# Two value projections by seven block products, and the gate sums of the linear attention moved behind them

## The reference, cut to what matters

```python
# stage "v": stick-breaking attention of the first block
q, k, v = jnp.split(x @ w_qkv, 3, axis=-1)      # v: 512 x 1024
# stage "od_v": gated linear attention of the second block
z = h @ w_in
q, k, v, r, ga = jnp.split(z, [hk, 2 * hk, 2 * hk + hv, 2 * hk + 2 * hv], axis=-1)   # v: 512 x 1024
log_a = jax.nn.log_sigmoid((ga @ w_a2 + b_a).astype(jnp.float32)) / C_TAU
b = jnp.cumsum(log_a, axis=3)                   # within chunks of 64 tokens
q_t, k_t, k_s = q * jnp.exp(b), k * jnp.exp(-b), k * jnp.exp(b_last - b)
```

## Time and profile before

| | us |
|---|---|
| Median of 3 runs | 2387.3 (2385.33 to 2389.44) |
| The profiled execution's own time | 2386.84 |
| Its span in the profile | 2385.0 |
| PE busy | 2340.6 (98%) |
| PEld busy | 2037.7 (85%) |
| DVE busy | 1587.9 (67%) |
| ACT busy | 1029.4 (43%) |
| POOL busy | 339.0 (14%) |

### The profile page before, as it was taken

One profiled execution on the slowest core, in us unless ns is written; L12 is line 12 of the kernel. 1 busy time (PEld: TensorE's weight loads), 2 busy tenths in 40 slices (PEclk: granted clock), 3 DMA queues, 4 the chain that ended last, 5 costly groups with the idle time before them and its releaser, 6 DMA issues.

```text
span 2385.0 us, 36878 instructions
## 1 busy us (share of the span) xinstructions
PE 2340.6 (98%) x14899; PEld 2037.7 (85%) x14899; DVE 1587.9 (67%) x2174; ACT 1029.4 (43%) x1352; POOL 339.0 (14%) x294
## 2 busy tenths in 40 slices
PE   7699999999999999999999999999999999999999
PEld 7688899988886678999878779999888877899987
DVE  8845877846536777777585546899534545799942
ACT  6421544532225725445234444556423344455622
POOL 6402000002002240000224241000121002000000
PEclk9899999999999999999999999999999999999999
DMA  2422333233232122332333313233332212333332
GB/s 58 104 97 90 105 107 105 83 101 113 89 99 69 40 94 85 107 103 82 96 107 110 89 64 114 82 105 89 101 102 85 93 66 71 89 107 107 85 107 85
DMA packets 328844, 219.67 MB, mean 92 GB/s; under 512 B 11188, under 2 KB 319050, under 8 KB 328618
## 3 DMA queue, kind: packets, MB, share of 16 engines
q1 hardware_dynamic: 322298, 208.46, 29.6%
q0 software_dynamic: 3024, 7.90, 1.4%
q10 hardware_dynamic: 3360, 1.02, 0.2%
HBM read 206.59 MB, written 2.10 MB: 87 GB/s over the span
## 4 chain that ended last, share of the span: by engine, by line
PE 90%; DVE 4%; POOL 3%; ACT 2%; issue 1%; SPq 0%; DMA 0%; DVEq 0%; ACTq 0%; POOLq 0%
PE psum L1380 9%; PE psum L1382 9%; PE psum L1381 9%; PE psum L1136 9%; PE psum L1138 9%; PE psum L1137 9%; PE psum L1349 3%; PE psum L1350 3%; PE psum L1351 3%; PE psum L1524 2%; PE psum L1525 2%; PE psum L1526 2%; PE psum L1248 1%; PE psum L1244 1%; PE psum L1245 1%; PE psum L1228 1%
## 5 line engine op out<-in xcount | busy, mean ns | idle before, releaser
L2093 ACT CAST w_hi<-w_stage 128x2048 fp32r<-128x2048 f32 x129 | 246.7, 1912 | 691.8 <-PE psum L1138 408.4
L2973 DVE TENSOR_TENSOR w_lo<-w_stage,w_hi 128x2048 fp32r<-128x2048 f32 x126 | 300.0, 2381 | 275.6 <-ACT w_hi L2093 275.6
L1380 PE MATMUL psum<-x_sum_hi,w_hi 128*128 128x256 f32 x1088 | 308.0, 283 | 0.2 <-issue 0.2
L1382 PE MATMUL psum<-x_sum_hi,w_lo 128*128 128x256 f32 x1088 | 307.9, 283 | 0.0
L1381 PE MATMUL psum<-x_sum_lo,w_hi 128*128 128x256 f32 x1088 | 307.9, 283 | 0.0
L2163 ACT CAST w_hi<-w_parts 128x1024 fp32r<-128x1024 f32 x204 | 213.3, 1049 | 200.9 <-PE psum L1382 111.1
L3101 DVE TENSOR_TENSOR w_lo<-w_parts,w_hi 128x1024 fp32r<-128x1024 f32 x204 | 248.1, 1219 | 51.7 <-ACT w_hi L2163 50.5
L1380 PE MATMUL psum<-x_hi,w_hi 128*128 128x256 f32 x816 | 230.9, 283 | 0.0
L1381 PE MATMUL psum<-x_lo,w_hi 128*128 128x256 f32 x816 | 230.9, 283 | 0.0
L1382 PE MATMUL psum<-x_hi,w_lo 128*128 128x256 f32 x816 | 230.9, 283 | 0.0
L1136 PE MATMUL psum<-hidden_raw_hi,w_hi 128*128 128x512 f32 x572 | 223.6, 391 | 0.3 <-DVE w_lo L2973 0.3
(11 more groups left out here) (584 smaller groups left out, 5283.5 us busy)
## 6 DMA issues: line engine op xcount, KB each, us to landing
w_stage<-in_ffn_w_down_dram SPq DMA_DIRECT2D x64, 704.0 KB, 4.6
w_parts<-in_ffn_w_gu_dram SPq DMA_DIRECT2D x144, 256.0 KB, 3.4
w_parts<-in_ffn_w_gate_dram SPq DMA_DIRECT2D x64, 256.0 KB, 3.1
w_parts<-in_ffn_w_up_dram SPq DMA_DIRECT2D x64, 256.0 KB, 3.1
w_stage<-in_sb_w_qkv_dram SPq DMA_DIRECT2D x12, 1024.0 KB, 5.1
w_stage<-in_od_w_in_dram SPq DMA_DIRECT2D x12, 1024.0 KB, 5.2
w_stage<-in_ev_w_in_dram SPq DMA_DIRECT2D x10, 1024.0 KB, 5.0
w_stage<-in_ssm_w_glu_dram SPq DMA_DIRECT2D x8, 1024.0 KB, 5.5
```

What stands on the lines that cost most here:

```text
L1380: nc.tensor.matmul(dst, hi, x_hi[:, k, :], start=(start and k == 0), stop=False, skip_group_check=True)
L1382: mm = nc.tensor.matmul(dst, lo, x_hi[:, k, :], start=False, stop=(k == DC // 2 - 1), skip_group_check=True)
L2093: nc.scalar.copy(whi[:, half, :], wst[:, half, :]).then_inc(whi_done, 1)
L2973: V.tensor_tensor(wlo[:, half, :], wst[:, half, :], whi[:, half, :].bitcast(F32), ALU.subtract).then_inc(wlo_done, 1)
```

## The change

1. `v` and `od_v` are no longer token stages of tiles. The weight W is cut in four blocks of 512 x 512, A_mj (m is the half of the output columns, j the half of the inner dimension), and x in four blocks B (inner half by token half of 256). Seven products of sums of these blocks are computed instead of eight of the blocks: S1 = A21 + A22, A11, S2 = S1 + A11, A12, S3 = A21 + A11, S4 = S2 + A12, A22, in this order on PE. A product is two token tiles of 12 matmuls on 512 columns, so a stage has 7 x 24 = 168 matmuls.
2. For each product ACT casts the weight sum (128 x 2048) and DVE subtracts; DVE also makes S1 to S4 (128 x 2048 each). The four sums of x (128 x 1024 each) are made by DVE from the residual for `v` (4 steps) and from `x_hi` and `x_lo` for `od_v` (7 steps at the end of `od_q`, 5 at the head of `od_k`); ACT casts them and DVE subtracts.
3. Layer norm 1 adds its bias to the residual on ACT (8 more passes of 128 x 512), which the sums of `v` need.
4. `log_decay` on ACT stands behind the copy of `gate_low` at once, ahead of the rounding of the sums. `cumulate` on DVE is cut in three and stands behind the last low part of `od_v` and the splits for `od_r`.
5. The scores of head 0 of `v` stand between the two token tiles of the last product, those of head 1 behind it, and they wait for the last copy of `v_tok` (before: for all but the last).

The core of the diff:

```diff
-        ("q", 2, 4, 4), ("k", 2, 4, 4), ("v", 2, 8, 4), ...
+        ("q", 2, 4, 4), ("k", 2, 4, 4), ("v", 0, 0, 0), ...
-        ("od_q", 1, 4, 4), ("od_k", 1, 4, 4), ("od_v", 2, 8, 4), ...
+        ("od_q", 1, 4, 4), ("od_k", 1, 4, 4), ("od_v", 0, 0, 0), ...
...
+            def token_loads(name):
...
+                sp.wait_ge(part_done, last.part0)
+                if name == "od_v":
+                    sp.wait_ge(ga_done, 1)
+                load(T_S3, 1, 0, whole, parts_landed[0])
+                load(T_A22, 1, 1, whole, parts_landed[0])
+                sp.wait_ge(wlo_done, ST[name].it0 * 2 - 1)
...
 # PE
+                arrived(T_S1, 1)
+                for tile in range(2):
+                    product(token_w, T_S1, tile, t1, True)
+                if name == "od_v":
+                    pe.wait_ge(la_link, GLA_HEADS)
+                arrived(T_A11)
+                for tile in range(2):
+                    product(token_x, T_A11, tile, x_part(0, 0), True)
+                arrived(T_S2, 2)
+                for tile in range(2):
+                    pe.wait_ge(copied, token_moved_count(name, 3 + tile))
+                    product(token_x, T_S2, tile, t2)
...
+                for tile in range(2):
+                    pe.wait_ge(added, token_moved_count(name, 3 + tile))
+                    product(token_x, T_A22, tile, t4)
+                    if tile == 0 and early is not None:
+                        early()
...
                 elif h == 1:
-                    pe.wait_ge(evac_done, ST["v"].evac1 - 1)
+                    pe.wait_ge(evac_done, ST["v"].evac1)
 # ACT
                 elif name == "od_k":
-                    split_stage(name)
                     log_decay()
+                    token_sums_and_first("od_v")
                 elif name == "od_v":
-                    split_stage(name)
+                    seven_token_stage(name, gvt)
                     decays()
 # DVE
+            def token_part_sum(name, n, dst, a, b):
+                a, b, dst = (token_part[name][k][:, :, :] for k in (a, b, dst))
+                token_step(name, TOKEN_STEPS[name] + n, V.tensor_tensor(dst, a, b, ALU.add))
+            def token_low(name, n):
+                dve.wait_ge(rounded, token_rounded_count(name, 4 + n + 1))
+                hi, lo = token_weights(name, n)
+                V.tensor_tensor(lo, token_part[name][n][:, :, :], hi.bitcast(F32), ALU.subtract).then_inc(low_ready, 1)
+            def token_first_parts(name):
+                dve.wait_ge(parts_landed[0], token_landed_count(name))
+                token_part_sum(name, 1, T_S1, T_S3, T_A22)
+                token_low(name, T_S1)
+                dve.wait_ge(parts_landed[1], token_landed_count(name))
+                token_part_sum(name, 2, T_S2, T_S1, T_A11)
+                token_part_sum(name, 3, T_S3, T_S3, T_A11)
+            def token_second_parts(name):
+                token_low(name, T_S2)
+                dve.wait_ge(a12_landed, token_a12_count(name))
+                token_part_sum(name, 4, T_S4, T_S2, T_A12)
+                token_low(name, T_A12)
...
+            def k_stage():
+                for half in range(2):
+                    for u in range(2):
+                        copy_unit("k", k_f, 1.0, 0, 2 * half + u)
+                    split(ST["k"].it0 + 1, half)
+                token_sums()
+                for u in range(2):
+                    copy_unit("k", k_f, 1.0, 1, u)
+                token_sum_lows("v")
+                token_first_parts("v")
+                for u in range(2):
+                    copy_unit("k", k_f, 1.0, 1, 2 + u)
             def v_stage():
+                token_low("v", T_A11)
+                token_second_parts("v")
...
+                token_put("v", v_t, 0)
+                stick_abs(0)
+                token_put("v", v_t, 1)
+                stick_soft(0)
...
+            def od_k_stage():
+                token_sums_late()
+                for u in range(2):
+                    copy_unit("od_k", gk, 1.0, 0, u)
+                token_sum_lows("od_v")
+                token_first_parts("od_v")
+                for u in range(2):
+                    copy_unit("od_k", gk, 1.0, 0, 2 + u)
+            def od_v_stage():
...
+                token_low("od_v", T_A22)
+                split(ST["od_v"].it0, 0)
+                token_put("od_v", gvt, 0)
+                token_put("od_v", gvt, 1)
+                split(ST["od_v"].it0, 1)
+                cumulate_gates()
+                for h in range(GLA_HEADS):
+                    cumulate_head(h)
+                cumulate_rest()
```

More of the change, by code:

```diff
@@ L506, in before, with tokens_before, sevens_before, iters_before @@
             return sum(SEVEN_ITERS[other] for other in list(SEVEN)[:list(SEVEN).index(name)])
+        def tokens_before(name):
+            return [other for other in TOKEN_STEPS if run.index(other) < run.index(name)]
+        def sevens_before(name):
+            return [other for other in SEVEN if run.index(other) < run.index(name)]
+        def iters_before(name):
+            return sum(SEVEN_ITERS[other] for other in sevens_before(name))
         def products_count(name, i, n):
-            return (before(name) + i) * PRODUCTS + n
+            return (before(name) + i) * PRODUCTS + 14 * len(tokens_before(name)) + n
@@ L537, in gated_count, with token_summed_count, token_moved_count @@
+        def token_summed_count(name, n):
+            steps = sum(X_STEPS[other] for other in sevens_before(name)) + iters_before(name) * 6
+            return steps + sum(TOKEN_STEPS[other] + 4 for other in tokens_before(name)) + n
+        def token_moved_count(name, n):
+            return iters_before(name) * 4 + 4 * len(tokens_before(name)) + n
         def gated_count(name, i, n):
@@ L610, in tile_source @@
                 return rows[:, :, bass.ds(i * 512 + col, 512)]
-            return wcols(t[w][0], i * 512 + half * 256 + col)
+            return wcols(t[w][0], i * 512 + (half * 256 + first * 512 + col))
         def tile_view(w, name, half):
@@ L1527, in token_products, with token_stage @@
                 return mm
[L1529 removed]
+            def token_stage(name, xh, xl):
                 st = ST[name]
[L1532 to L1543 removed]
+                for half in range(2):
+                    pe.wait_ge(wlo_done, st.it0 * 2 + half + 1)
+                    for n in range(TT):
+                        token_products(bank[4 + n], name, half, n, xh, xl).then_inc(part_done, 1)
@@ L2445, in pair_high, with round_token_sums @@
                 nc.scalar.copy(hhi[:, p, :], bank[7]).then_inc(o_hi, 1)
-            def v_stage():
-                st = ST["v"]
-                for i in range(st.iters):
-                    for half in range(2):
-                        if i < st.iters - 1 or half == 0:
-                            split(i + st.it0 + 1, half, i * st.parts + st.part0 + st.parts // 2 * (half + 1))
+            def round_token_sums(name):
+                for n, made in ((0, 1), (2, 2), (1, 3), (3, 4)) if name == "v" else ((2, 3), (3, 7), (0, 10), (1, 12)):
+                    act.wait_ge(summed, token_summed_count(name, made))
+                    nc.scalar.copy(token_sum_hi[name][n][:, :, :], token_sum[name][n][:, :, :]).then_inc(rounded, 1)
@@ new lines, in token_sums_late, with token_sum_lows @@
+            def token_sums_late():
+                t1, t2, t3 = (token_sum["od_v"][n][:, :, :] for n in range(3))
+                b11 = token_high_low(0, 0)
+                token_difference(8, t1, b11, token_high_low(0, 1))
+                token_step("od_v", 11, V.scalar_tensor_tensor(t2, t3, -1.0, b11[0], ALU.mult, ALU.subtract))
+                token_step("od_v", 12, V.tensor_tensor(t2, t2, b11[1], ALU.subtract))
+            def token_sum_lows(name):
+                for n, count in enumerate((1, 3, 2, 4) if name == "v" else (3, 4, 1, 2)):
+                    dve.wait_ge(rounded, token_rounded_count(name, count))
+                    V.tensor_tensor(token_sum_lo[name][n][:, :, :], token_sum[name][n][:, :, :],
+                                    token_sum_hi[name][n][:, :, :].bitcast(F32), ALU.subtract).then_inc(x_low, 1)
@@ L3812, in cumulate, with od_q_stage @@
                                 ALU.subtract).then_inc(cum_done, 1)
+            def od_q_stage():
+                for half in range(2):
+                    for u in range(2):
+                        copy_unit("od_q", gq, 128 ** -0.5, 0, 2 * half + u)
+                    split(ST["od_k"].it0, half)
+                token_sums_early()
+            def od_k_stage():
[4 more added lines that the diff above has]
+                token_first_parts("od_v")
+                for u in range(2):
+                    copy_unit("od_k", gk, 1.0, 0, 2 + u)
+            def od_v_stage():
+                token_low("od_v", T_A11)
+                token_second_parts("od_v")
+                for tile in range(2):
+                    token_seed("od_v", tile)
+                token_low("od_v", T_S3)
```

(5 more changed lines are left out.)

303 lines of the change are left out of this document (239 added, 64 removed).

## The result

The changed kernel takes 2399.1 us (median of 5 runs, 2397.45 to 2400.58), the kernel before 2387.6 in the runs beside it: a ratio of 1.0048, 95% interval 1.0035 to 1.0061. That is 11.5 us more. The forecast was 8.3 us more. The profiled execution took 2397.72 us (span 2395.9), 10.9 more than the profiled one of before, and this 10.9 is what the trace can explain.

The account below looks back on a forecast made before the run. PE's own stream was taken to bound the kernel (90% of the chain). 1.9 (`v`) + 5.4 (`od_v`) + 1.1 (`od_r`) = 8.4 us over the profiled 2386.84 gave 2395.2, said as 2395.6; range 2389 to 2401.

Parts of the forecast that it names:

- matmuls saved, both stages: In `v` and `od_v`, 192 matmuls become 168 each, 5.44 us off each stage, 10.9 us for both.
- wait ahead of S1, `v`: PE is ready for the first product of `v` at 687.64, its low part at 688.8: 1.2 us of wait.
- wait ahead of A11, `v`: PE waits 4.2 us for A11's low part, behind S2, S3, two copies and the gain reductions on DVE.
- stick attention late: Behind `v`, the absolute value of head 1 begins 1.9 us late, and nothing gives this back: +1.9 us.
- wait ahead of S1, `od_v`: PE waits 8.5 us for the first product, as ACT rounds the sums only after the log decay.
- `od_v` altogether: PE ends the stage's products at 1906.35 instead of 1900.99: +5.4 us, the slow clock in S1 nearly all hidden.
- scores of `od_r`: Running sums stand behind everything on DVE, so the first scores of `od_r` wait 1.1 us (0 to 2).
- the clock also falls in v's wait of 4.2 us: Rival: PE's clock drops in the wait ahead of A11, up to 2.5 us more, 2397.7; chance 0.22.
- The rival of the other side: Operands of both stages stand in time, so the waits ahead of their first products vanish: 2379.4 us; chance 0.11.
- Costs put at nothing: Layer norm 1's eight bias passes fit ACT's idle time; q and k swaps, 6 us later, still have 30 us.
- the slack at A12: In `v`, A12's low part stands at 708.9 where PE asks at 709.4, the tightest operand behind A11.

Follow-up runs that it names:

- e4: The changed kernel with DVE's and ACT's work for both stages reordered, each product's own low part ahead of later sums, log decay passes split by casts: 2380.0 us.
- e1: The changed kernel with spare matmuls on PE, 15 between S1 and A11 of `v` and 37 ahead of S1 of `od_v`: 2399.1 us.
- after: The changed kernel itself, without any follow-up edit: 2399.1 us, its profiled run 2397.72.
- e3: The changed kernel with ACT rounding the four sums of x for `od_v` ahead of the log decay: 2394.5 us, median of seven widely scattered runs.
- e6: e4 with 3 or 4 spare matmuls in front of each of PE's first four waits in the stick attention: 2379.3 us.
- e10: e9 without any of the spare matmuls that kept PE busy in the stick attention: 2377.8 us.
- e5: e4 with the running sums of the gates moved among DVE's low parts of `od_v`, the gate pass ahead of A12's: 2380.7 us.
- e2: The changed kernel with, only in `v`, DVE making the low part of A11 right behind that of S1: 2395.9 us.
- e9: e4 with S4 ahead of S3, running sums among later low parts, head 0's soft part ahead of `v`'s last copies, spare matmuls in the stick attention: 2376.6 us.

## Why the prediction was right, and where it was short

Slower was right, the time lay in the range, and each wait was in its place, with its cause and nearly its size. What was short is the clock.

| term | forecast | measured |
|---|---|---|
| matmuls saved, both stages | -10.9 | -10.9 (e4: 168 slots in 38.08 us) |
| wait ahead of S1, `v` | 1.2 | 1.24 |
| wait ahead of A11, `v` | 4.2 | 3.93 |
| clock in `v` | 0 (rival: up to 2.5) | 1.6 |
| stick attention late | 1.9 | 0.87 + 1.21 |
| clock in the stick attention | not thought of | 1.3 |
| wait ahead of S1, `od_v` | 8.5 | 8.54 |
| `od_v` altogether | +5.4 | +5.53 |
| scores of `od_r` | 1.1 | 1.07 |

**The step that failed** is the one that put "the clock also falls in v's wait of 4.2 us" among the rivals, at 0.22, and the forecast at full clock. It fell, at 699.2, 1.3 us after work had begun again, and e1 shows its price with everything else as it was: 1.6 us, where I had bounded it by 2.5. My reason against it was that PE may never have been at full clock ahead of the slow pair of the earlier trace rows. The trace of after shows that it had been. The same place there, with full clock ahead of the wait (3.31 us) and about half behind it:

```profile
17.00:20.00 3.00, 0.16 (x1) 0.16 (x2) 2.86 (x9) 1.87 (x5) 1.27 (x2) 1.00 0.22 44
20.00:24.00 4.00, 4.00 (x21) 3.83 (x22) 3.90 (x9) 3.00 (x6) 3.84 (x4) 0.57 0.00 0
```

By the Trainium skill ("TensorE: Matmul & The Clock Gate", section "Why this matters for your kernels") the wait was a gap to avoid, and the trace agrees here. The rule does not sort the shorter waits of these runs: 2.38 us brought the clock down in e1, 2.37 us did not in e3.

**The second miss** is that waits of 0.87, 1.06 and 1.02 us, which end at 735.33, 741.43 and 742.95, took the clock down in the stick attention. Head 2 to head 3 took 7.41 us instead of 6.09: 1.3.

```profile
741.43 0.50 PE L1711 MATMUL psum<-not_past,ident_rounded 128*128 128x512 f32 x1 [1.06 <-ACT stick L2595]
...
742.95 0.37 PE L1717 MATMUL psum<-q_feat,k_feat 64*128 64x128 f32 x1 [1.02 <-ACT stick L2595]
```

Before the change two such waits stood there and the clock held. e6 takes the spell away by keeping PE busy, e10 by taking the wait of 1.06 us away: both point at the idle time of PE. Since e10's remaining waits, 0.88, 1.02 and 1.02 us, also lie further apart, no run tells whether their number or their spacing counts. With 1.6 and 1.3 added to 8.4, less the 0.4 that the stretch up to `od_v` gave back and the 0.45 of the start, the sum is 10.5 for the 10.9 measured.

**`od_v`.** The 8.5 us of wait come from the log decay ahead of the casts (e3: 7.3 of them), and the slow S1 cost nothing, since the low part of A11 came no earlier. e1 tested that: S1 at full pace, and PE waited 2.38 us instead of 0.63 ahead of A11.

**The rival of the other side** ("the operands are in time", 2379.4) was wrong for this kernel, and its number was met by another order: e4, with nothing changed but the order, came to 2380.0. It reckoned with full clock in the stick attention, which the profiled run of e4 did not have, so the agreement is in part luck. The products were worth what they save, and their order cost 19 us. My argument against this rival, that the chain from the last gate matmul has no room before 1857.1, held only with the log decay ahead of the casts. The sums do not depend on it, and with the passes set apart by the casts everything fits.

**Costs put at nothing.** The bias passes of layer norm 1 and the swaps of q and k left no wait; the slack at A12, put at 0.5 us, was 0.45 in `v` (the low part ends at 710.09, PE comes at 710.54), and in `od_v` there was no wait either. e5 shows how little room it is: 1.15 us of work beyond idle time and slack became 1.2 us of wait.

## What to carry to other kernels

When a change makes PE's work shorter, lay out by hand the order of the engine that feeds it ahead of the first two operands: DVE, busy 69% of the span, was 1.2 to 8.5 us late with these operands (the 8.5 because ACT fed it late). Put first what the next product needs (its own low part before the sums of later ones), and work with a distant deadline (gain reductions, log decay) into gaps that are longer than it. And count a wait of PE at more than its length: several short ones close together can cost the clock as well.

## What the runs showed of the hardware

- The clock fell behind a wait, not only in it: after 3.93 us of idling the first matmuls of A11 ran at full pace (starts about 0.24 us apart from the second on), and from 699.55 on seven steps from start to start were 0.43.
- Equal waits do not have equal effect: 2.38 us (e1) at half clock behind it, 2.37 us (e3) not, 1.67 us (e2) not; and at the same place of the program 2.81 us (e10) at half clock behind it, 2.85 us (e9) not. What decides is open. In the stick attention the clock fell in all six profiles with waits of about 0.87, 1.05 and 1.02 us close together (after and e1 to e5: 735.33, 741.43 and 742.95 in after), and not with two waits of 1.02 us (before), nor with waits of 0.88, 1.02 and 1.02 us about 6 us apart (e10).
- With that spell, head 2 to head 3 took 7.4 us in three of these profiles (after, e3, e5) and 8.9 to 9.0 in three (e1, e2, e4), for the same instructions. What decides between the two is open.
